# Opening of layer 0 in chunks of 2, 2, 4, 4, 2 and 2 k tiles, with the gate matrices loaded behind it

## The chip, the cores and the metric

One core of one Trainium2 chip. The metric is the time of one execution on the device, in microseconds (us), the median of three runs. One further execution was recorded by the profiler; all rows below are from it.

## What is computed

Two mixer layers over 256 latent and 256 context tokens of width 2048, then a last RMSNorm. All in float32. What matters here is how a layer begins:

```python
shift, scale, gate = jnp.split(c_act @ w_ada + b_ada, 3, axis=-1)
h = rmsnorm(x, norm_g) * (1 + scale) + shift
u = h @ w_in
```

`w_ada` is 2048 x 6144 for each layer, and the vectors `c_act` and `cc_act` (latent and context tokens) are multiplied by it. The 2048 inputs of `h` are 16 k tiles of 128. Behind it come a Conformer convolution, a gated linear recurrence (RG-LRU, whose small gate matrices are block diagonal), attention, and the output product.

## The kernel before

Everything is transposed: channels on the 128 partitions, the 512 tokens along the free axis. The product with `w_in` runs in blocks of 128 output columns, over 16 k tiles. Each float32 factor is split in two fp32r parts, and three matmuls of 128x512 are made per block and k tile (lines 559 to 561 in the opening, 614 to 616 behind it): high times high, high of the weights with low of h, low of the weights with high of h. ScalarE makes the high part of the weights (`w_hi`, line 803), VectorE subtracts it for the low part (`w_lo`, line 1077), in units of up to 1024 columns; there are 4 buffers for units, and the w_hi of unit u waits until the matmuls of unit u - 4 are done.

**The opening of layer 0.** The first seven blocks cannot wait for all of `c_act @ w_ada`. So they are made together, k tiles outside, each block in a PSUM bank of its own. A chunk is 2 k tiles of all seven blocks; 8 chunks. For a chunk these steps follow each other:

- `ada0_mm` (L512, matmuls at L523): `c_act` times the columns of `w_ada` of the chunk's k tiles, for scale and shift, in 4 pieces of 1 MB (scale 0 and 1, then shift 0 and 1), summed in one bank. A piece is here 1024 rows by 256 columns, 8 matmuls of 256 columns, each 1 KB run of memory one row of the transfer.
- ScalarE copies that bank (`ada0_rows`, L817), TensorE transposes it (`ada0_tp`, L531), VectorE sums and adds the bias (`ada0_out`, L1085 to L1096).
- For each k tile, VectorE makes `T` (L1128), ScalarE `h_hi` (L844), VectorE `h_lo` (L1135).
- The chunk's weights, one load of 896 KB (7 blocks by 256 columns), make two units, of 4 and of 3 blocks.
- TensorE runs 14 steps (`mm_chunk`, L542), a step being one block and one k tile: blocks 0 to 3 for both k tiles, then 4 to 6. Behind steps 1 and 3 it puts the two shift pieces of the *next* chunk, behind step 6 the transposes of the next chunk, behind steps 10 and 12 the two scale pieces of the chunk after that. `ada0_mm` for a chunk may start only when VectorE has summed the chunk before.

**The stream.** SyncE issues all weight loads from one list (`stream`, L158), in order. In the opening there are 40, numbered here from 0: per chunk three pieces, the weights, the last piece. They use 6 slots of 1 MB in rotation: three of `raw`, one in `glu`, two in `qreg`. So a load waits for the release of the load six before it (`used`, L309): for a piece its matmuls, for a chunk's weights the w_lo of the last unit made from them. Behind the opening the stream goes on with three slots (load 40 is the weights of block 7, load 41 those of block 8). There a piece of `w_ada` is 128 rows by 2048 columns, in 8 KB rows, and takes 4 matmuls of 512 columns (L501, 8 instructions); the opening of layer 1, at about 870 us, loads its weights in 2 KB rows. A waiting issue holds up all issues behind it. The matrices of the gates of the recurrence (`gate_weights`, L412, issues at L420, 4 loads of 128 KB in 256-byte rows) are issued behind load 32.

**VectorE's and ScalarE's order in a chunk.** VectorE: sums, T of the first k tile, w_lo of the first unit, T of the second, both h_lo, w_lo of the second unit. ScalarE: the copy of the bank, w_hi of the first unit, h_hi, w_hi of the second, h_hi.

The release of a chunk of weights and the slots, as the code has them:

```python
SLOT = [i % (NRAW + 3) if i < opened else (i - opened) % NRAW for i in range(len(STREAM))]
if SLOT[i] in SLOT[:i]:
    sp.wait_ge(*used(i - 1 - SLOT[:i][::-1].index(SLOT[i])))
if item[0] == "chunk":
    return C.at("lo", chunk_unit(item[1], False))
```

Of the kernel before, what the change touches and what calls it, by code (L numbers as in the profile page):

```python
# [21 lines left out]
ALU = mybir.AluOpType  # L22
# [42 lines left out]
CK = 2  # L65
CHUNKS = DT // CK
FRONT = 4
# [54 lines left out]
LEAD = 2  # L122
ADA0_AT, TP_AT, LEAD_AT = (1, 3), 6, (10, 12)


def ada0(c):

    return [("ada0", kind, c, g) for kind in (SCL, SHIFT) for g in range(2)]
# [6 lines left out]

SHIFTED = 2 * CHUNKS - 2 * OPEN[0]

# [6 lines left out]
def chunk_unit(c, front):  # L144

    return 2 * c + (0 if front else 1)
# [5 lines left out]


def chunk_blocks(front):
    return range(FRONT) if front else range(FRONT, OPEN[0])


def stream():  # L158

    plan = ada_plan()  # L160
    s = []
    for c in range(CHUNKS):
        first = ada0(c)
        s += first[:3] + [("chunk", c)] + first[3:]
    s += [("w", b) for b in (OPEN[0], OPEN[0] + 1)]
    for l in range(LAYERS):
        for b in range(OPEN[l], NB):
# [44 lines left out]
def program(nc, io, known):  # L212
    ctx = ExitStack()
    with ctx:
# [94 lines left out]
        def used(i):  # L309

            item = STREAM[i]
            if item[0] == "w":
                return C.at("lo", unit(0, item[1], 1))
            if item[0] == "chunk":
                return C.at("lo", chunk_unit(item[1], False))
            if item[0] == "open":
                return C.at("lo", quarter_unit(item[1], SIDE // 2 - 1))
            if item[0] == "pw":
                return C.at("pw_mm", item[1], CT - 1)
            return C.at(item[0] + "_mm", *item[1:])  # L320

        def source(u):

            if u < 2 * CHUNKS:
                c, back = divmod(u, 2)
                return ("chunk", c), slice(back * FRONT * CK * P, (OPEN[0] if back else FRONT) * CK * P)
# [6 lines left out]
        def block_done(gb):  # L333

            l, b = divmod(gb, NB)
            if b >= OPEN[l]:
                return C.at("mm", unit(l, b, 1))
            return C.at("mm", quarter_unit(3, b // 2) if l else chunk_unit(CHUNKS - 1, b < FRONT))
# [69 lines left out]
        def _(sp):  # L408
# [22 lines left out]
            for i, item in enumerate(STREAM):  # L431
# [5 lines left out]
                elif item[0] == "chunk":  # L437
                    src = io["w_blocks"][0:OPEN[0], :, item[1] * CK * P:(item[1] + 1) * CK * P].rearrange("b p c -> p b c")
                    dst = dst[:, 0:OPEN[0] * CK * P].rearrange("p (b c) -> p b c", b=OPEN[0])
# [4 lines left out]
                elif item[0] == "ada0":  # L444
                    kind, c, g = item[1:]
                    at0 = kind * D + c * CK * P
                    src = io["w_ada"][0, g * D // 2:(g + 1) * D // 2, at0:at0 + CK * P].rearrange("(j p) c -> p j c", p=P)
                    dst = dst.rearrange("p (j c) -> p j c", j=DT // 2)
# [9 lines left out]
                if i == 2 * DT:  # L458
                    gate_weights(0)
# [30 lines left out]
        def _(pe):  # L490
# [21 lines left out]
            def ada0_mm(kind, c, g):  # L512
# [4 lines left out]
                n = CK * P  # L517
# [3 lines left out]
                for j in range(8):  # L521
                    r = 32 * (j % 4)
                    last = mm(psA[r:r + 32, 0:n], rows[:, g * 8 + j, :], w[:, j * n:(j + 1) * n],  # L523
                              start=(kind == SCL and g == 0 and j < 4), stop=(kind == SHIFT and g == 1 and j >= 4),
                              tile_position=(0, r))
                last.then_inc(*C.up("ada0_mm", kind, c, g))

            def ada0_tp(c):
                pe.wait_ge(*C.at("ada0_rows", c))
                for j in range(CK):  # L530
# [11 lines left out]
            def mm_chunk(c):  # L542
# [3 lines left out]
                for front in (True, False):  # L546
                    u = chunk_unit(c, front)
                    pe.wait_ge(*C.at("lo", u))
                    for i in range(CK):
                        k = c * CK + i  # L550
                        if front:
                            pe.wait_ge(*C.at("h_lo", 0, k))
                        for n, b in enumerate(chunk_blocks(front)):
# [3 lines left out]
                            at = (n * CK + i) * P  # L557
# [177 lines left out]
            for item in ada0(1)[:LEAD]:  # L735
# [58 lines left out]
        def _(act):  # L794
# [20 lines left out]
            def ada0_rows(c):  # L815
                act.wait_ge(*C.at("ada0_mm", SHIFT, c, 1))
                fn(T[:, 6, 0:CK * P], psA[:, 0:CK * P], ACT.Copy).then_inc(*C.up("ada0_rows", c))  # L817
# [145 lines left out]
            for gb in range(GLOB):  # L963
                l, b = divmod(gb, NB)
                if b == 0:
# [3 lines left out]
                    if l == 0:  # L969
                        rms_std(l)  # L970
                        for c in range(CHUNKS):
                            if c:
                                ada0_rows(c)
                            hi(chunk_unit(c, True))
                            if c == 0:
                                hi(chunk_unit(c, False))
                                ada0_rows(c)
                            modulate(l, c * CK)
                            if c:
                                hi(chunk_unit(c, False))  # L980
                            modulate(l, c * CK + 1)
# [79 lines left out]
        def _(dve):  # L1061
# [18 lines left out]
            def ada0_out(c):  # L1080

                dve.wait_ge(*C.at("ada0_tp", c))
                ps = psA[:, 0:CK * P].rearrange("p (q j r) -> p r q j", q=CK, j=4)
                for kind, rows in ((SCL, slice(0, 2)), (SHIFT, slice(2, 4))):
                    V.tensor_reduce(tiny[:, 1 + kind, 0:2 * CK].rearrange("p (r q) -> p r q", r=2), ps[:, rows], axis=AX.X,  # L1085
                                    op=ALU.add).then_inc(*C.up("ada0_sum", kind, c))
                dve.wait_ge(*C.ago("ada0_sum"))
                for kind in (SCL, SHIFT):
                    at = kind * DT + c * CK
                    for i in range(2):  # L1090
                        V.tensor_tensor(ada[:, 0, i, at:at + CK], tiny[:, 1 + kind, CK * i:CK * i + CK], b_ada[:, 0, at:at + CK],
                                        ALU.add).then_inc(*C.up("ada_out", 0, kind, c))
# [401 lines left out]
```

## Time and profile before

| | |
|---|---|
| median of 3 runs | 1322.59 us (1319.38 to 1323.63) |
| the profiled execution | 1322.9 us, its span 1321.1 us |
| TensorE matmul busy | 1258.6 us, 95% of the span |
| VectorE, ScalarE busy | 733.7 us (56%), 534.6 us (40%) |
| share of TensorE in the chain that ended last | 83% |
| moved by DMA | 233.73 MB, mean 177 GB/s |

How to read it: times are us from the start of the span. The chain of waits follows, from the last instruction back, what released each step. A row of a timeline has start, duration, engine, line, operation, output and inputs, the count, and in brackets the idle time before it with what ended it. The duration of a matmul reaches to its modelled end; the distance between two starts is what one takes in a row of them. The granted clock of TensorE is given as a share of 2.4 GHz.

### The profile page before, as it was taken

What the parts mean: (1) busy time and instruction counts of PE and PEld (TensorE: products, weight loads), DVE (VectorE), ACT (ScalarE), POOL (GpSimd) and SP (SyncE); (2) the same over time, 40 slices, a digit from 0 to 9 for tenths busy, and PEclk for the clock granted to TensorE, in tenths of its full rate; (3) what the DMA queues carried; (4) which work ended last, traced back from release to release, by engine and by line L of the source; (5) the groups of instructions that cost most, each with busy time, mean ns of one, the idle gap of its engine ahead of it and who ended that gap; (6) DMA issues with size and microseconds to landing.
All of it is one profiled execution on the core that took longest, in us unless ns stands there. A gap on an engine that the chain in (4) does not pass through costs nothing.

```text
span 1321.1 us, 17033 instructions
## 1 busy us (share of the span) xinstructions
PE 1258.6 (95%) x7004; PEld 970.9 (73%) x7004; DVE 733.7 (56%) x1188; ACT 534.6 (40%) x843; POOL 8.2 (1%) x10
## 2 busy tenths in 40 slices
PE   3798999999999999999999999989999999999996
PEld 1465777767777777776777777758887998889995
DVE  3443436687565555552343233385789976755554
ACT  5222344452223334453332122244665554565452
POOL 0000100000000000000000000000000000000000
PEclk9999999999999999999999999989999999999998
DMA  9999655446443333333454554453332433325541
GB/s 343 332 320 324 220 201 212 191 192 263 155 187 128 128 127 127 128 128 134 169 225 175 213 208 173 186 191 104 120 131 93 160 128 128 128 96 192 182 169 64
DMA packets 76317, 233.73 MB, mean 177 GB/s; under 512 B 8016, under 2 KB 50128, under 8 KB 54352
## 3 DMA queue, kind: packets, MB, share of 16 engines
q1 hardware_dynamic: 76240, 232.65, 49.0%
q8 instruction: 55, 0.90, 0.3%
q14 instruction: 22, 0.18, 0.0%
HBM read 230.54 MB, written 2.10 MB: 176 GB/s over the span
## 4 chain that ended last, share of the span: by engine, by line
PE 83%; DVE 7%; DMA 5%; ACT 3%; issue 1%; SPq 0%; DVEq 0%; ACTq 0%
PE psum_block L614 21%; PE psum_block L615 20%; PE psum_block L616 20%; PE psum_ada L501 5%; PE psum_scores L691 3%; PE psum_scores L648 2%; PE psum_scores L669 2%; DMA raw<-in_w_ada 2%; DVE w_lo L1077 2%; DMA Y<-in_xT 1%; PE psum_scores L682 1%; DMA qreg<-in_w_ada 1%; DVE T L1128 1%; DVE h_lo L1135 1%; DMA glu<-in_w_ada 1%
## 5 line engine op out<-in xcount | busy, mean ns | idle before, releaser
L614 PE MATMUL psum_block<-h_hi,w_hi 128*128 128x512 f32 (+1 forms) x1616 | 562.4, 348 | 0.7 <-ACT glu L1050 0.7
L615 PE MATMUL psum_block<-h_lo,w_hi 128*128 128x512 f32 (+1 forms) x1616 | 547.9, 339 | 0.0
L616 PE MATMUL psum_block<-h_hi,w_lo 128*128 128x512 f32 (+1 forms) x1616 | 547.7, 339 | 0.0
L1077 DVE TENSOR_TENSOR w_lo<-raw,w_hi 128x1024 fp32r<-128x1024 f32 x218 | 263.4, 1218 | 398.6 <-ACT w_hi L803 398.4
L803 ACT ACTIVATE w_hi<-raw 128x1024 fp32r<-128x1024 f32 x218 | 228.5, 1053 | 530.1 <-PE psum_block L616 516.2
L614 PEld LDWEIGHTS psum_block<-h_hi,w_hi 128*128 128x128 f32 x1616 | 306.3, 190 | 78.1 <-issue 38.7
L615 PEld LDWEIGHTS psum_block<-h_lo,w_hi 128*128 128x128 f32 x1616 | 306.6, 190 | 35.3 <-issue 3.8
L616 PEld LDWEIGHTS psum_block<-h_hi,w_lo 128*128 128x128 f32 x1616 | 306.4, 190 | 34.2
L1276 DVE SCALAR_TENSOR_TENSOR Y<-glu,small,Y 128x512 f32<-128x512 f32 (+1 forms) x240 | 130.4, 612 | 0.0
L501 PE MATMUL psum_ada<-raw,cstat 128*32 128x512 f32 x512 | 67.2, 616 | 5.4 <-DMA raw<-in_w_ada 5.4
L917 ACT ACTIVATE T<-psum_scores,stats 128x512 f32<-128x512 f32 (+1 forms) x48 | 28.9, 615 | 52.7 <-DVE stats L1301 52.7
L844 ACT ACTIVATE h_hi<-T,ada 128x256 fp32r<-128x256 f32 x64 | 28.7, 501 | 45.4 <-DVE T L1128 45.4
L1085 DVE TENSOR_REDUCE tiny<-psum_ada 128x4 f32<-128x16 f32 x16 | 2.0, 169 | 71.3 <-PE psum_ada L531 71.3
L523 PE MATMUL psum_ada<-raw,cstat 128*32 128x256 f32 x272 | 20.5, 424 | 21.1 <-DMA raw<-in_w_ada 21.1
L691 PE MATMUL psum_scores<-T,v 128*128 128x512 f32 x80 | 36.4, 593 | 1.4 <-ACT T L932 1.4
L501 PEld LDWEIGHTS psum_ada<-raw,cstat 128*32 128x32 f32 x512 | 11.5, 109 | 34.5 <-issue 26.5
L831 ACT ACTIVATE T<-Y 128x512 f32<-128x512 f32 (+1 forms) x48 | 26.1, 550 | 22.4 <-DVE Y L1201 13.3
L648 PE MATMUL psum_scores<-T,bd 128*128 128x512 f32 x64 | 30.7, 625 | 3.9 <-DVE T L1234 3.9
L923 ACT ACTIVATE T<-T,stats 128x512 f32<-128x512 f32 (+1 forms) x48 | 27.3, 640 | 13.6 <-DVE stats L1311 13.6
L1234 DVE SCALAR_TENSOR_TENSOR T<-qreg,small,T 128x512 f32<-128x512 f32 x48 | 32.5, 745 | 0.0
L523 PEld LDWEIGHTS psum_ada<-raw,cstat 128*32 128x32 f32 x272 | 7.7, 118 | 32.5 <-issue 16.1
L669 PE MATMUL psum_scores<-kT,qreg 128*128 128x512 f32 x64 | 31.4, 611 | 0.0
(174 smaller groups left out, 1105.6 us busy)
## 6 DMA issues: line engine op xcount, KB each, us to landing
raw<-in_w_blocks SPq DMA_DIRECT2D x105, 1024.0 KB, 4.8
raw<-in_w_ada SPq DMA_DIRECT2D x81, 1024.0 KB, 5.5
qreg<-in_w_ada SPq DMA_DIRECT2D x10, 1024.0 KB, 11.2
glu<-in_w_ada SPq DMA_DIRECT2D x5, 1024.0 KB, 9.7
Y<-in_xT SPq DMA_DIRECT2D x4, 1024.0 KB, 12.4
T<-in_xT SPq DMA_DIRECT2D x16, 256.0 KB, 7.2
raw<-in_w_blocks SPq DMA_DIRECT2D x4, 896.0 KB, 11.4
raw<-in_pw SPq DMA_DIRECT2D x2, 1024.0 KB, 6.2
```

Source lines behind the costliest of these rows:

```text
L501: last = mm(psA[32 * j:32 * j + 32, :], cstat[:, k, 2:34], w[:, j * TOK:(j + 1) * TOK], start=(k == 0), stop=(k == DT - 1), tile_position= ...
L614: mm(ps[:, 0:n], hi, hh[:, k, t], start=(at == 0), stop=False)
L615: mm(ps[:, 0:n], hi, hl[:, k, t], start=False, stop=False)
L616: last = mm(ps[:, 0:n], lo, hh[:, k, t], start=False, stop=(at == DT - 1))
L648: last = mm(psS[:, 2 * d + g, :], bd[:, g, d * CT + t, :], T[:, 4 * d, :], start=True, stop=True)
L669: mm(psS[:, g, :], qt, kT[:, kv, :], start=True, stop=False)
L691: last = mm(psS[:, 0, :], v[:, kt, kv * HD:(kv + 1) * HD], T[:, 4 + kt, :], start=(kt == first), stop=(kt == 3))
L803: fn(wh[:, u % 4, 0:cols.stop - cols.start], raw_of(item)[:, cols], ACT.Copy).then_inc(*C.up("hi", u))
L917: fn(T[:, g, k0:TOK], psS[:, g, k0:TOK], ACT.Exp, scale=SCALE, bias=st[:, 1, g:g + 1], accum_out=st[:, 2, g:g + 1]).then_inc(*C.up("att_ex ...
L1077: V.tensor_tensor(wl[:, u % 4, 0:n], raw_of(item)[:, cols], wh[:, u % 4, 0:n].bitcast(F32), ALU.subtract).then_inc(*C.up("lo", u))
L1234: stt(out, x, lcw[:, c, k:k + 1], out, ALU.mult, ALU.add).then_inc(*C.up("taps", l, t, d))
L1276: stt(out, x, dwh[:, c:c + 1], out, ALU.mult, ALU.add).then_inc(*C.up("conv", l, t, k))
```

## The change

The opening is cut in 6 chunks of 2, 2, 4, 4, 2 and 2 k tiles. In a chunk of 4, a piece of `w_ada` is 512 rows by 512 columns (2 KB rows, 4 matmuls of 512 columns), and there are 8 pieces; the weights are two loads, blocks 0 to 3 (1 MB) and 4 to 6 (768 KB), in 2 KB rows too, and make four units, of 2, 2, 2 and 1 blocks. Chunks of 2 are loaded as before. There are again 40 loads: 0 to 9 as before; 10 to 15, 18 and 19 the pieces of chunk 2, 16 and 17 its weights; 20 to 25, 28 and 29 the pieces of chunk 3, 26 and 27 its weights; then two chunks of 5 loads.

`beside` places the pieces among TensorE's steps: the scale pieces of the chunk after next from 4 steps behind the transposes on, one a step; the shift pieces of the next chunk spread over the steps ahead of the transposes. This gives, for chunks 0 to 4: shift at steps 2, 4; 1, 2, 3, 4; 4, 8, 12, 16; 6, 13; 2, 4. Transposes behind step 6; 6; 20; 20; 6. Scale at 10 to 13; 10 to 13; 24, 25; 24, 25; none.

VectorE takes w_lo of the first unit ahead of the sums, and all the other w_lo of the chunk behind its last h_lo. ScalarE takes w_hi of the second unit behind the second h_hi. The gate matrices are issued behind load 40.

```diff
-CK = 2
-CHUNKS = DT // CK
-FRONT = 4
+SPAN = (2, 2, 4, 4, 2, 2)
+CHUNKS = len(SPAN)
+LOADS = {2: (range(0, 7),), 4: (range(0, 4), range(4, 7))}
+WORK = {2: (range(0, 4), range(4, 7)), 4: (range(0, 2), range(2, 4), range(4, 6), range(6, 7))}
+UNITS0 = [(c, n) for c in range(CHUNKS) for n in range(len(WORK[SPAN[c]]))]
...
-LEAD = 2
-ADA0_AT, TP_AT, LEAD_AT = (1, 3), 6, (10, 12)
...
-    return [("ada0", kind, c, g) for kind in (SCL, SHIFT) for g in range(2)]
+    return [("ada0", kind, c, g) for kind in (SCL, SHIFT) for g in range(SPAN[c])]
...
-SHIFTED = 2 * CHUNKS - 2 * OPEN[0]
+SHIFTED = len(UNITS0) - 2 * OPEN[0]
...
-def chunk_unit(c, front):
-    return 2 * c + (0 if front else 1)
+def chunk_k(c):
+    return sum(SPAN[:c])
+def chunk_unit(c, n):
+    return UNITS0.index((c, n))
+def chunk_units(c):
+    return range(chunk_unit(c, 0), chunk_unit(c, 0) + len(WORK[SPAN[c]]))
+def beside(c):
+    tp = OPEN[0] * SPAN[c] - 8
+    late = ada0(c + 1)[SPAN[c + 1]:] if c + 1 < CHUNKS else []
+    ahead = ada0(c + 2)[:SPAN[c + 2]] if c + 2 < CHUNKS else []
+    steps = {(i + 1) * tp // (len(late) + 1): item for i, item in enumerate(late)}
+    steps.update({tp + 4 + i: item for i, item in enumerate(ahead)})
+    return tp, steps
...
-        s += first[:3] + [("chunk", c)] + first[3:]
+        early = len(first) - SPAN[c] // 2
+        s += first[:early] + [("chunk", c, n) for n in range(len(LOADS[SPAN[c]]))] + first[early:]
...
-                return C.at("lo", chunk_unit(item[1], False))
+                c, blocks = item[1], LOADS[SPAN[item[1]]][item[2]]
+                return C.at("lo", max(chunk_unit(c, n) for n, w in enumerate(WORK[SPAN[c]]) if w[0] in blocks))
...
-            if u < 2 * CHUNKS:
-                c, back = divmod(u, 2)
-                return ("chunk", c), slice(back * FRONT * CK * P, (OPEN[0] if back else FRONT) * CK * P)
+            if u < len(UNITS0):
+                c, n = UNITS0[u]
+                blocks, cols = WORK[SPAN[c]][n], SPAN[c] * P
+                m = next(m for m, load in enumerate(LOADS[SPAN[c]]) if blocks[0] in load)
+                first = blocks[0] - LOADS[SPAN[c]][m][0]
+                return ("chunk", c, m), slice(first * cols, (first + len(blocks)) * cols)
...
-                    src = io["w_blocks"][0:OPEN[0], :, item[1] * CK * P:(item[1] + 1) * CK * P].rearrange("b p c -> p b c")
-                    dst = dst[:, 0:OPEN[0] * CK * P].rearrange("p (b c) -> p b c", b=OPEN[0])
+                    blocks, cols, at0 = LOADS[SPAN[item[1]]][item[2]], SPAN[item[1]] * P, chunk_k(item[1]) * P
+                    src = io["w_blocks"][blocks[0]:blocks[-1] + 1, :, at0:at0 + cols].rearrange("b p c -> p b c")
+                    dst = dst[:, 0:len(blocks) * cols].rearrange("p (b c) -> p b c", b=len(blocks))
...
-                    at0 = kind * D + c * CK * P
-                    src = io["w_ada"][0, g * D // 2:(g + 1) * D // 2, at0:at0 + CK * P].rearrange("(j p) c -> p j c", p=P)
-                    dst = dst.rearrange("p (j c) -> p j c", j=DT // 2)
+                    rows, cols, at0 = D // SPAN[c], SPAN[c] * P, kind * D + chunk_k(c) * P
+                    src = io["w_ada"][0, g * rows:(g + 1) * rows, at0:at0 + cols].rearrange("(j p) c -> p j c", p=P)
+                    dst = dst.rearrange("p (j c) -> p j c", c=cols)
...
-                if i == 2 * DT:
+                if item == ("w", OPEN[0]):
                     gate_weights(0)
...
-                n = CK * P
+                n, count = SPAN[c] * P, DT // SPAN[c]
                 rows = cstat[:, :, 2:34] if kind == SCL else cstat[:, :, 0:32]
                 if g == 0 and kind == SCL and c:
                     pe.wait_ge(*C.at("ada0_sum", SHIFT, c - 1))
-                for j in range(8):
+                for j in range(count):
                     r = 32 * (j % 4)
-                    last = mm(psA[r:r + 32, 0:n], rows[:, g * 8 + j, :], w[:, j * n:(j + 1) * n],
-                              start=(kind == SCL and g == 0 and j < 4), stop=(kind == SHIFT and g == 1 and j >= 4),
-                              tile_position=(0, r))
+                    last = mm(psA[r:r + 32, 0:n], rows[:, g * count + j, :], w[:, j * n:(j + 1) * n],
+                              start=(kind == SCL and g == 0 and j < 4),
+                              stop=(kind == SHIFT and g == SPAN[c] - 1 and j >= count - 4), tile_position=(0, r))
...
                 step = 0
-                for front in (True, False):
-                    u = chunk_unit(c, front)
+                tp, steps = beside(c)
+                for u, blocks in zip(chunk_units(c), WORK[SPAN[c]]):
                     pe.wait_ge(*C.at("lo", u))
-                    for i in range(CK):
-                        k = c * CK + i
-                        if front:
+                    for i in range(SPAN[c]):
+                        k = chunk_k(c) + i
+                        if blocks[0] == 0:
                             pe.wait_ge(*C.at("h_lo", 0, k))
-                        for n, b in enumerate(chunk_blocks(front)):
+                        for n, b in enumerate(blocks):
                             if k == 0 and b == 2:
                                 pe.wait_ge(*C.at("rms_std", 0))
                             ps = bank(b)
-                            at = (n * CK + i) * P
+                            at = (n * SPAN[c] + i) * P
                             hi, lo = wh[:, u % 4, at:at + P], wl[:, u % 4, at:at + P]
                             mm(ps, hi, hh[:, k, :], start=(k == 0), stop=False)
                             mm(ps, hi, hl[:, k, :], start=False, stop=False)
                             last = mm(ps, lo, hh[:, k, :], start=False, stop=(k == DT - 1))
-                            if i == CK - 1 and b == chunk_blocks(front)[-1]:
+                            if i == SPAN[c] - 1 and b == blocks[-1]:
                                 last.then_inc(*C.up("mm", u))
-                            if step in ADA0_AT and c + 1 < CHUNKS:
-                                ada0_mm(*ada0(c + 1)[LEAD + ADA0_AT.index(step)][1:])
-                            if step == TP_AT and c + 1 < CHUNKS:
+                            if step in steps:
+                                ada0_mm(*steps[step][1:])
+                            if step == tp and c + 1 < CHUNKS:
                                 ada0_tp(c + 1)
-                            if step in LEAD_AT and c + 2 < CHUNKS:
-                                ada0_mm(*ada0(c + 2)[LEAD_AT.index(step)][1:])
                             step += 1
...
                         for c in range(CHUNKS):
-                            if c:
-                                ada0_rows(c)
-                            hi(chunk_unit(c, True))
-                            if c == 0:
-                                hi(chunk_unit(c, False))
-                                ada0_rows(c)
-                            modulate(l, c * CK)
-                            if c:
-                                hi(chunk_unit(c, False))
-                            modulate(l, c * CK + 1)
+                            units = chunk_units(c)
+                            hi(units[0])
+                            ada0_rows(c)
+                            for i in range(2):
+                                modulate(l, chunk_k(c) + i)
+                            hi(units[1])
+                            for i in range(2, SPAN[c]):
+                                modulate(l, chunk_k(c) + i)
+                                hi(units[i])
...
             def h_chunk(c):
-                k = c * CK
-                if k:
-                    dve.wait_ge(*C.at("h_lo", 0, k - 1))
-                modulate(0, k)
-                lo(chunk_unit(c, True))
-                modulate(0, k + 1)
+                for k in range(chunk_k(c), chunk_k(c) + SPAN[c]):
+                    if k >= 2:
+                        dve.wait_ge(*C.at("h_lo", 0, k - 2))
+                    modulate(0, k)
+                    if k > chunk_k(c):
+                        h_lo(0, k - 1)
                 h_lo(0, k)
-                h_lo(0, k + 1)
-                lo(chunk_unit(c, False))
...
                         for c in range(CHUNKS):
+                            lo(chunk_units(c)[0])
                             ada0_out(c)
                             h_chunk(c)
+                            for u in chunk_units(c)[1:]:
+                                lo(u)
```

The sums of `ada0_out` and the copy of `ada0_rows` take the width of the chunk in the same way.

## Rows read from the trace of the kernel before

**Rows 1.** The page, part 2: GB/s in 40 slices of 33 us

```profile
GB/s 343 332 320 324 220 201 212 191 192 263 155 187 128 128 127 127 128 128 134 169 225 175 213 208 173 186 191 104 120 131 93 160 128 128 128 96 192 182 169 64
```

**Rows 2.** TensorE's waits from 38 to 164 us; engines' busy time from 164 to 857 us

```profile
PE psum_ada L523 <- DMA raw<-in_w_ada: 5.1, 4, 2.2
PE psum_ada L523 <- DMA qreg<-in_w_ada: 4.2, 2, 3.4
PE psum_ada L523 <- DMA glu<-in_w_ada: 3.3, 2, 2.9
...
164.00:857.00 693.00, 693.00 (x3172) 500.98 (x3174) 345.47 (x488) 241.28 (x378) 1.85 (x1) 1.00 0.46 174
```

**Rows 3.** Waits of SyncE's DMA queue from 38 to 164 us

```profile
SPq L454 <- DVE w_lo L1077: 56.0, 9, 11.4
```

**Rows 4.** The chain from 67 us on: start, duration, what

```profile
66.97 0.27 DVE tiny L1085 x2
...
67.94 0.88 DVE T L1128 x2
68.82 1.14 DVE w_lo L1077
69.96 0.79 DVE T L1128 x2
70.75 1.58 DVE h_lo L1135 x4
72.33 0.88 DVE w_lo L1077
...
73.23 5.39 DMA raw<-in_w_ada
...
119.69 8.25 DMA qreg<-in_w_ada
```

**Rows 5.** TensorE's timeline in chunk 3: start, duration, what

```profile
100.47 1.07 PE L523 MATMUL psum_ada<-raw,cstat 128*32 128x256 f32 x16
...
102.06 0.40 PE L561 MATMUL psum_scores<-h_hi,w_lo 128*128 128x512 f32 x1
102.29 0.40 PE L559 MATMUL psum_scores<-h_hi,w_hi 128*128 128x512 f32 x1
...
103.08 1.07 PE L523 MATMUL psum_ada<-raw,cstat 128*32 128x256 f32 x16
```

**Rows 6.** The chain behind the opening: two pieces of 512 columns

```profile
175.26 1.85 PE psum_ada L501 x16
```

**Rows 7.** DMA in 40 slices of 56 to 120 us, then of 868 to 874 us

```profile
GB/s 252 268 371 355 350 348 349 346 348 348 94 108 372 359 356 349 349 349 348 348 266 264 380 352 349 349 350 353 348 349 141 328 373 350 349 350 346 350 294 203
...
GB/s 437 382 382 423 437 396 382 382 382 328 205 273 341 341 396 396 382 423 396 355 410 382 396 355 382 451 410 451 273 232 314 259 396 55 546 55 601 109 710 164
```

**Rows 8.** The chain's transfers at 56 and 141 us; landing of the load issued at 157.9

```profile
56.27 7.05 DMA raw<-in_w_ada
...
140.57 5.21 DMA glu<-in_w_ada
...
DMA to landing us min/median/max: 5.1/5.1/5.1
```

**Rows 9.** TensorE after two idles (timeline), the chain at 134 us, granted clock at 128

```profile
46.41 1.07 PE L523 MATMUL psum_ada<-glu,cstat 128*32 128x256 f32 x16 [2.94 <-DMA glu<-in_w_ada]
...
127.98 1.94 PE L523 MATMUL psum_ada<-qreg,cstat 128*32 128x256 f32 x16 [3.38 <-DMA qreg<-in_w_ada]
...
134.05 0.23 PE psum_ada L531 x2
...
128.00:130.00 2.00, 2.00 (x17) 0.73 (x17) 0.00 (x0) 0.01 (x1) 0.00 (x0) 0.50 1.10 349
```

**Rows 10.** The first matmul of block 7 on TensorE

```profile
163.77 0.39 PE L614 MATMUL psum_block<-h_hi,w_hi 128*128 128x512 f32 x1
```

**Rows 11.** The issues of the gate matrices: duration ns min/median/max

```profile
L420 SPq DMA_DIRECT2D bd<-in_lru_w x4: 1352/1676/2942, 109.8 to 116.2; - x4
```

More of the change, by code:

```diff
@@ L118, in ada_plan @@
     return plan
-LEAD = 2
-ADA0_AT, TP_AT, LEAD_AT = (1, 3), 6, (10, 12)
 def ada0(c):
-    return [("ada0", kind, c, g) for kind in (SCL, SHIFT) for g in range(2)]
+    return [("ada0", kind, c, g) for kind in (SCL, SHIFT) for g in range(SPAN[c])]
 def opening(quarter):
     return [("open", quarter)]
-SHIFTED = 2 * CHUNKS - 2 * OPEN[0]
+SHIFTED = len(UNITS0) - 2 * OPEN[0]
 def unit(l, b, j):
     return SHIFTED + 2 * (l * NB + b) + j
-def chunk_unit(c, front):
-    return 2 * c + (0 if front else 1)
+def chunk_k(c):
[11 more added lines that the diff above has]
+    return tp, steps
 def quarter_unit(quarter, pair):
     return unit(1, 0, 0) + quarter * SIDE // 2 + pair
-def chunk_blocks(front):
-    return range(FRONT) if front else range(FRONT, OPEN[0])
 def stream():
@@ L337, in block_done @@
                 return C.at("mm", unit(l, b, 1))
-            return C.at("mm", quarter_unit(3, b // 2) if l else chunk_unit(CHUNKS - 1, b < FRONT))
+            if l:
+                return C.at("mm", quarter_unit(3, b // 2))
+            last = CHUNKS - 1
+            return C.at("mm", chunk_unit(last, next(n for n, w in enumerate(WORK[SPAN[last]]) if b in w)))
         def bank(gb):
@@ L529, in ada0_tp @@
                 pe.wait_ge(*C.at("ada0_rows", c))
-                for j in range(CK):
+                for j in range(SPAN[c]):
                     last = nc.tensor.transpose(psA[:, j * P:(j + 1) * P], T[:, 6, j * P:(j + 1) * P], ident)
@@ L734, in _ @@
             ada0_tp(0)
-            for item in ada0(1)[:LEAD]:
+            for item in ada0(1)[:SPAN[1]]:
                 ada0_mm(*item[1:])
@@ L815, in ada0_rows @@
             def ada0_rows(c):
-                act.wait_ge(*C.at("ada0_mm", SHIFT, c, 1))
-                fn(T[:, 6, 0:CK * P], psA[:, 0:CK * P], ACT.Copy).then_inc(*C.up("ada0_rows", c))
+                act.wait_ge(*C.at("ada0_mm", SHIFT, c, SPAN[c] - 1))
+                fn(T[:, 6, 0:SPAN[c] * P], psA[:, 0:SPAN[c] * P], ACT.Copy).then_inc(*C.up("ada0_rows", c))
             def square(l, m):
@@ L1082, in ada0_out @@
                 dve.wait_ge(*C.at("ada0_tp", c))
-                ps = psA[:, 0:CK * P].rearrange("p (q j r) -> p r q j", q=CK, j=4)
+                n, k = SPAN[c], chunk_k(c)
+                ps = psA[:, 0:n * P].rearrange("p (q j r) -> p r q j", q=n, j=4)
                 for kind, rows in ((SCL, slice(0, 2)), (SHIFT, slice(2, 4))):
-                    V.tensor_reduce(tiny[:, 1 + kind, 0:2 * CK].rearrange("p (r q) -> p r q", r=2), ps[:, rows], axis=AX.X,
+                    V.tensor_reduce(tiny[:, 1 + kind, 0:2 * n].rearrange("p (r q) -> p r q", r=2), ps[:, rows], axis=AX.X,
                                     op=ALU.add).then_inc(*C.up("ada0_sum", kind, c))
@@ L1088, in ada0_out @@
                 for kind in (SCL, SHIFT):
-                    at = kind * DT + c * CK
+                    at = kind * DT + k
                     for i in range(2):
-                        V.tensor_tensor(ada[:, 0, i, at:at + CK], tiny[:, 1 + kind, CK * i:CK * i + CK], b_ada[:, 0, at:at + CK],
+                        V.tensor_tensor(ada[:, 0, i, at:at + n], tiny[:, 1 + kind, n * i:n * i + n], b_ada[:, 0, at:at + n],
                                         ALU.add).then_inc(*C.up("ada_out", 0, kind, c))
-                ck = slice(c * CK, (c + 1) * CK)
                 dve.wait_ge(*C.ago("ada_out"))
                 for i in range(2):
-                    stt(A[:, 0, i, ck], ada[:, 0, i, SCL * DT + c * CK:SCL * DT + (c + 1) * CK], 1.0,
-                        norm_g[:, 0, ck], ALU.add, ALU.mult).then_inc(*C.up("A", 0, i))
+                    stt(A[:, 0, i, k:k + n], ada[:, 0, i, SCL * DT + k:SCL * DT + k + n], 1.0,
+                        norm_g[:, 0, k:k + n], ALU.add, ALU.mult).then_inc(*C.up("A", 0, i))
                 dve.wait_ge(*C.ago("A"))
```

## The prediction

> **What bounds the kernel now.** I read the slices of the page first. The first four, 132 us and nearly all of the opening of layer 0, move 320 to 343 GB/s, where the later ones mostly move 60 to 260 [rows 1]: only here is the DMA near what it can bring. The waits say what that costs: from 38 to 164 us TensorE waits for pieces of w_ada for 5.1 + 4.2 + 3.3 = 12.6 us, and from 164 to 857 us it is busy for 693.00 of 693.00 us [rows 2]. So what the opening gains or loses reaches the end of the kernel whole: nothing behind it can take time back.
>
> Who holds the transfers up is in SyncE's waits: 56.0 us for w_lo in the opening [rows 3]. A load takes the slot of the load six before it. The slot of a piece of w_ada comes free with its matmuls, but that of a chunk of weights only with VectorE's last w_lo from it, behind the whole modulation of that chunk. The chain of chunk 2 shows this ring: sums from 66.97, modulation, the last w_lo at 72.33, the issue at 73.23, landing 5.39 us later [rows 4]. Three turns take from 73.23 to 119.69, 15.5 us each, and TensorE's own work in a chunk is 14 steps of 0.69, four pieces of 1.22 and 0.26 of transposes, 14.8 us. The step is three matmuls 0.23 apart; the piece is 103.08 - 100.47 less two steps [rows 5]. So at present the load that waits for w_lo is the last piece of the next chunk, one per turn, and the turn hides nearly all of it.
>
> **The prices.** A piece of 512 columns: two take 1.85 us, so 0.93, and with the 0.15 that a lone piece has on top of its 1.07 it is 1.08 (0.15 is 1.22 less the row's 1.07) [rows 5, 6]. A megabyte in 1 KB rows goes at 349 GB/s, 3.0 us; in 2 KB rows (the opening of layer 1) mostly at 382 to 396, 2.65 us [rows 7]. A load that finds the queue empty lands 5.2 to 5.4 us after its issue, one in 8 KB rows after 5.1 [rows 4, 8]; I take 5.1 for 2 KB rows and 5.4 for 1 KB rows. The clock: after an idle of 3.38 us TensorE ran at 1.2 GHz from 127.98 to 134.05, 6.1 us, and lost 3.0; after 2.94 us it lost nothing, the piece behind it took the 1.07 of the full clock [rows 9]. VectorE from the transposes to the last w_lo: now 6.26 us (66.97 to 73.23). A chunk of 2 k tiles has w_lo of 1.14 in front instead, and the second w_hi behind both h_hi, so 5.6. A chunk of 4 needs, up to the w_lo that ends the first weight load, 0.97 for the sums, 4 x 0.83 of T, 4 x 0.79 of h_lo, about 1.2 of waits for h_hi and 1.14 of w_lo: 9.8 us [rows 4].
>
> **The new order.** The loads are numbered from 0 as they are issued. Up to load 9 they are the same; 10 to 19 are chunk 2 (16 and 17 its weights), 20 to 29 chunk 3, 30 on chunks 4 and 5. Two things change for slots. Load 14, still behind w_lo of chunk 1, is now one of eight pieces that TensorE wants *during* chunk 1 (14, 15, 18, 19 at its steps 1 to 4). And loads 22 and 23, the pieces that TensorE wants at steps 12 and 13 of chunk 1, take the slots of 16 and 17: the weights of chunk 2, which are not released until chunk 2 is modulated.
>
> - Chunk 0: load 9 lands at 46.6 (46.4 now, a w_hi later), its piece ends 47.8, two steps and the transposes 49.4, then 7 steps and 4 pieces: 58.6. Loads 10 to 13 land by 46.6 + 4 x 2.65 = 57.2. Load 14 is issued at 49.4 + 5.6 = 55.0 and lands 59.9; then 15 at 62.5, 16 65.2, 17 (three quarters) 67.2, 18 69.8, 19 72.5.
> - Chunk 1: at step 3, 64.3, TensorE waits for load 18 until 69.8: **5.5 us idle**. Pieces, three steps and transposes would end at 75.2; at the low clock 77.3.
> - Load 22 waits for w_lo of chunk 2: 77.3 + 9.8 = 87.1, landing 92.2. TensorE is at that piece at 77.3 + 6 x 0.69 + 2 x 1.08 = 83.6: **8.6 us idle**.
> - Piece and step 13 at the low clock end at 95.7. Only now may ScalarE overwrite the w_hi buffer of the fourth unit of chunk 2; w_hi and w_lo of 512 columns are 0.65 each, load 23 is issued at 97.0 and lands at 102.1: **6.4 us idle**. Its piece ends at 104.2.
> - Chunk 2: 28 x 0.69 + 4 x 1.08 + 2 x 1.22 + 0.26 + 2.0 of low clock = 28.4, to 132.6, no wait (load 29 lands by 102.1 + 5.75 x 2.65 = 117.3).
> - Chunk 3: load 32 waits for chunk 3's first weights: transposes at 125.3, + 9.8 + 5.4 = 140.5; TensorE is there at 137.4, 3.1 us idle. Then 21 steps, 4 pieces, transposes: 160.2.
> - Chunk 4: 12.4, to 172.6. Chunk 5: 14 steps, 9.7, to 182.3. Block 7 now begins at 163.77 [rows 10], so the opening is **18.5 us longer**.
>
> **The gate matrices.** Their four small loads (issues of up to 2.94 us [rows 11]) stand between loads 32 and 33 and make one turn, from 119.69 to 140.57, 20.9 instead of 15.5 us, clock included [rows 4, 8]; that 5.4 us is saved and is already in the sum above, which has no such hole. In their new place they go out at about 160 and are first used behind block 8, which begins 11 us (16 steps) after 182.3. Behind them stands load 41, the weights of block 8: issued by about 168, it lands by 174. Cost nothing. The reorder of w_hi and w_lo in chunks of 2 costs nothing beyond the 0.2 above.
>
> The profiled execution took 1322.9, of it 1321.1 span; the median is 0.3 lower. 1322.6 + 18.5 = **1341 us**.
>
> **Bounds.** Row rate: 3.0 us per MB (no better than now) adds 3.1 in chunk 1 and little later; 410 GB/s takes 1. Lone landing: up to 7.05 [rows 8] adds 2 to 5, less where loads queue. Clock: if the idles of 3.1 us too drop it, 3 more; if none does, 6 to 7 less. So 1334 to 1349 for this case.
>
> The Trainium skill (DMA: Bandwidth & Descriptors, Anatomy of one DMA) fits a GpSimd-issued DMA as 2.0 us plus bytes by 436 GB/s, an estimate of 4.4 us for 1 MB: by that the three lone landings would give 2 us back, 1339. The rows show 5.1 at best, and the sum goes by them.
>
> **Rivals.**
> 1. *Slots do not bind; the rate does.* Then the 5.4 us of the gate loads go, at most 6.3 us of the other waits (12.6 less 3.4 of that turn and the first 2.9), and 16 x 0.14 of pieces: 1309 at best, about **1313**. For it: the DMA is full for most of the opening. Against it: 56.0 us of SyncE's waits are w_lo, and loads 22 and 23 are later in the slot order than chunk 2's weights. It decides if these two are issued before 75 us. 7 in 100. This is the other side; within 0.3% (about what a measurement can tell from no change), 2 in 100.
> 2. *The waits come, the clock holds.* 3.38 us is the only drop of the opening, and it may be chance. **1335**, 12 in 100.
> 3. *2 KB rows run like 1 KB rows.* Loads 10 to 19 then take 3.0 us per MB and the first idle is 8.6: **1344**, 5 in 100, since 382 to 396 GB/s stands in the rows against 349. (The Trainium skill, same page, Specifications, puts line rate at 512 B and more, by which doubling 1 KB rows brings nothing; the trace disagrees.)
> 4. The sum as above, 74 in 100.
>
> Faster 0.07, same 0.02, slower 0.91. The range leaves out rival 1 and the same-time case, and takes the bounds of the rest: 1332 to 1350.
>
> **What would show it.** In the profile after: SyncE waits for w_lo in two long stretches, about 20 us before load 22 (near 87) and some 9 before load 23; TensorE idle for w_ada near 64 to 70, 84 to 92, 96 to 102 and 137 to 140, some 24 us in all; 1.2 GHz after each of the first three; DMA almost idle from about 78 to 87; block 7 beginning near 182; no gate load in the opening. It is wrong if TensorE's idle in chunk 1 is under 10 us, or if block 7 begins before 164.

## The result and the profile after

| kernel | median us | against the kernel before (95% interval) |
|---|---|---|
| before, beside it | 1321.46 (1319.38 to 1323.63) | |
| changed | 1342.23 (1340.42 to 1343.38) | 1.0156 (1.0136 to 1.0175) |

The change makes the kernel 20.8 us slower. The page of the changed kernel, part 2 (TensorE's granted clock in tenths, and GB/s, in 40 slices of 33.5 us):

```profile
PEclk9978999999999999999999999989999999999998
...
GB/s 345 341 171 275 272 165 228 221 188 226 214 188 126 126 126 151 130 107 148 141 237 172 187 212 211 179 183 94 158 98 91 158 147 137 126 95 180 175 180 63
```

Against [rows 1] the high rates of the opening now spread over five slices instead of four, and the third slice moves 171 GB/s where its neighbours move 341 and 275. The clock is down in slices 3 and 4 (0.7 and 0.8). TensorE's and SyncE's waits in the opening (in all, how often, the longest):

```profile
PE psum_ada L544 <- DMA qreg<-in_w_ada: 14.3, 2, 7.5
PE psum_ada L544 <- DMA raw<-in_w_ada: 7.6, 2, 5.5
PE psum_ada L544 <- DMA glu<-in_w_ada: 5.2, 2, 3.4
```

```profile
SPq L475 <- DVE w_lo L1095: 84.6, 9, 19.7
SPq L475 <- PE psum_ada L544: 18.7, 9, 3.8
```

There are 27.1 us of waits for w_ada (14.3 + 7.6 + 5.2) instead of 12.6 [rows 2], and 84.6 us of SyncE's waits for w_lo instead of 56.0 [rows 3]. TensorE's timeline, the pieces it waited for and the first matmul of block 7:

```profile
46.66 1.20 PE L544 MATMUL psum_ada<-glu,cstat 128*32 128x256 f32 x16 [3.44 <-DMA glu<-in_w_ada]
...
65.73 1.06 PE L544 MATMUL psum_ada<-glu,cstat 128*32 128x512 f32 x8 [1.74 <-DMA glu<-in_w_ada]
...
73.19 1.93 PE L544 MATMUL psum_ada<-raw,cstat 128*32 128x512 f32 x8 [5.50 <-DMA raw<-in_w_ada]
...
94.54 1.93 PE L544 MATMUL psum_ada<-qreg,cstat 128*32 128x512 f32 x8 [7.51 <-DMA qreg<-in_w_ada]
...
104.80 1.94 PE L544 MATMUL psum_ada<-qreg,cstat 128*32 128x512 f32 x8 [6.75 <-DMA qreg<-in_w_ada]
...
141.75 1.07 PE L544 MATMUL psum_ada<-raw,cstat 128*32 128x256 f32 x16 [2.09 <-DMA raw<-in_w_ada]
...
184.45 0.39 PE L633 MATMUL psum_block<-h_hi,w_hi 128*128 128x512 f32 x1
```

These are loads 9, 15, 18, 22, 23 and 32. A duration of 1.93 for a piece is the low clock, one of 1.07 the full; behind the pieces at 46.66 and 141.75 the clock fell a little after they began. Block 7 begins at 184.45, 20.7 us behind [rows 10], and in the 693 us behind it nothing changes: TensorE is busy for 693.00 us again, as in [rows 2]; that is the last line here (each line: busy time of PE, PEld, DVE, ACT, POOL, granted clock, DMA share, GB/s):

```profile
48.00:50.00 2.00, 2.00 (x5) 1.61 (x6) 0.00 (x0) 0.29 (x1) 0.00 (x0) 0.50 1.05 387
74.00:76.00 2.00, 2.00 (x10) 0.83 (x3) 0.00 (x0) 0.00 (x0) 0.00 (x0) 0.50 1.05 386
80.00:84.00 4.00, 4.00 (x25) 2.54 (x23) 3.37 (x14) 1.56 (x4) 0.00 (x0) 1.00 0.01 4
84.00:88.00 4.00, 3.02 (x18) 1.13 (x14) 3.94 (x10) 3.64 (x7) 0.00 (x0) 1.00 0.00 2
144.00:146.00 2.00, 2.00 (x6) 1.63 (x5) 0.00 (x0) 0.00 (x0) 0.00 (x0) 0.50 1.05 349
184.00:877.00 693.00, 693.00 (x3171) 501.44 (x3173) 344.90 (x487) 241.46 (x378) 1.85 (x1) 1.00 0.46 174
```

The granted clock is 0.50, 1.2 GHz, behind the idles, and from 80 to 88 us the DMA moves almost nothing (4 and 2 GB/s) while TensorE runs dry at 87. Why stands in the chain of waits and in the timeline of VectorE and ScalarE:

```profile
58.82 14.32 DMA raw<-in_w_ada
...
88.20 1.15 DVE w_lo L1095
89.36 5.13 DMA qreg<-in_w_ada
...
99.53 5.23 DMA qreg<-in_w_ada
...
135.35 1.15 DVE w_lo L1095
136.51 5.20 DMA raw<-in_w_ada
```

```profile
80.51 0.29 DVE L1104 TENSOR_REDUCE tiny<-psum_ada 128x8 f32<-128x32 f32 x2 [9.79 <-PE psum_ada L552]
...
98.15 0.63 ACT L822 ACTIVATE w_hi<-qreg 128x512 fp32r<-128x512 f32 x1 [10.50 <-PE psum_misc L582]
98.81 0.69 DVE L1095 TENSOR_TENSOR w_lo<-qreg,w_hi 128x512 fp32r<-128x512 f32 x1 [8.34 <-ACT w_hi L822]
```

The sums of chunk 2 begin at 80.51; behind its modulation VectorE makes the w_lo that releases the first load of weights, from 88.20 on; only then, at 89.36, load 22 is issued, and it lands 5.13 us later. (The row at 58.82 is load 18, to which the section on the prediction comes back.) Load 23 waits for the w_lo at 98.81, which waits for the w_hi at 98.15, which waited 10.5 us for TensorE's last step of chunk 1. Load 32 repeats the first of these at 135.35. This is the ring of [rows 4] with one difference: what now stands six loads behind the weights of chunk 2 is a piece that TensorE wants before chunk 2 begins.

Last, the transfers of 56 to 80 us, nearly all in 2 KB rows:

```profile
GB/s 24 14 55 113 331 382 413 403 440 375 389 386 393 382 389 389 386 393 389 386 386 389 382 382 386 386 389 386 393 386 389 386 396 382 382 382 389 382 174 24
```

That is mostly 382 to 393, about 386 GB/s or 2.72 us for 1 MB, against 349 in 1 KB rows [rows 7].

### The profile page after: what moved, and what is told of

Same layout as the page of the kernel before. It is cut to its first block, busy times and chain, and to the rows that moved or that the text cites. A ratio compares the mean times of both kernels' runs of the same rounds, so it can differ in the third digit from the quotient of the medians.

```text
span 1341.2 us, 16753 instructions
## 1 busy us (share of the span) xinstructions
PE 1263.2 (94%) x6876; PEld 969.3 (72%) x6876; DVE 733.4 (55%) x1172; ACT 534.3 (40%) x841; POOL 8.2 (1%) x10
## 4 chain that ended last, share of the span: by engine, by line
PE 85%; DVE 5%; DMA 4%; ACT 3%; issue 1%; SPq 0%; DVEq 0%; ACTq 0%
PE psum_block L633 20%; PE psum_block L634 20%; PE psum_block L635 20%; PE psum_ada L522 4%; PE psum_scores L710 3%; PE psum_scores L688 2%; PE psum_scores L667 2%; DMA raw<-in_w_ada 2%; PE psum_ada L544 2%; DMA Y<-in_xT 1%; PE psum_scores L701 1%; PE psum_scores L580 1%; PE psum_scores L581 1%; PE psum_scores L582 1%; DVE w_lo L1095 1%
## 5 line engine op out<-in xcount | busy, mean ns | idle before, releaser
L544 PE MATMUL psum_ada<-raw,cstat 128*32 128x256 f32 (+1 forms) x224 | 23.1, 524 | 23.2 <-DMA raw<-in_w_ada 23.2
L1256 DVE SCALAR_TENSOR_TENSOR qreg<-qreg,T 128x512 f32<-128x512 f32 x16 | 10.3, 688 | 36.1 <-ACT qreg L922 36.1
```

Of the source, the lines that this page charges most:

```text
L544: last = mm(psA[r:r + 32, 0:n], rows[:, g * count + j, :], w[:, j * n:(j + 1) * n], start=(kind == SCL and g == 0 and j < 4), stop=(kind = ...
```

## The experiments

Theory: the weights of a chunk of 4 sit in the slots that pieces of the next chunk need (two long idles and a short one), and chunk 1 wants twice the pieces before its transposes (one idle); the low clock adds to both. The rivals are named with each run. Each ratio below is to the kernel before, run beside that experiment on the same chip; its median there was 1321.8 (e1 to e4), 1322.8 (e5, e6, e8, e9) and 1322.7 (e10), against 1321.46 beside the change. "The change" is 1342.23, and differences to it are differences of medians, so they are good to 1 or 2 us only.

**e1, the gate matrices alone.** The kernel before, with

```diff
-                if i == 2 * DT:
+                if item == ("w", OPEN[0]):
                     gate_weights(0)
```

> The kernel before with one edit: the gate matrices are issued behind load 40, as in the change. Theory (slot ring, the gate loads being a hole of their own): the turn of 20.9 us becomes 15.5, about 5.5 us less than before, 1316. Rival (the gate loads were hidden beside the ring, TensorE's wait there had another cause): 1321 to 1322.

1317.63 us, 0.9972 (0.9961 to 0.9984): 4.2 us less (2 to 5 by the interval), and not the 5.5 expected. From its timeline, the piece of load 9, and block 7:

```profile
45.90 1.94 PE L523 MATMUL psum_ada<-glu,cstat 128*32 128x256 f32 x16 [3.04 <-DMA glu<-in_w_ada]
...
159.35 0.39 PE L614 MATMUL psum_block<-h_hi,w_hi 128*128 128x512 f32 x1
```

The gate hole is gone. Block 7 begins at 159.35, 4.4 us earlier than [rows 10]. The clock fell behind the first idle, of 3.04 us instead of 2.94 [rows 9], but that cost little here: the piece of load 14 comes at 63.83 instead of 63.37, since its own wait shrank from 2.19 to 0.37 us. The two turns around the hole, from the piece at 109.84 to the one at 145.82, took 36.0 us, and take 31.2 in e1 (110.23 to 141.41): 4.8 us are gained, and 0.4 lost ahead of them. Of the 5.4 priced, 0.6 comes back as a wait, since the piece at 145.82 waited 0.33 us and the one at 141.41 waits 0.90.

**e2, no chunks of 4.** The changed kernel with

```diff
-SPAN = (2, 2, 4, 4, 2, 2)
+SPAN = (2, 2, 2, 2, 2, 2, 2, 2)
```

> The changed kernel with SPAN all 2: new orders of w_hi and w_lo, steps 2, 4, 10 and 11 for the pieces, gates behind, but no chunk of 4. Theory (only the slots of the weights of chunks of 4 and the eight pieces asked for in chunk 1 cost): 1312 to 1315, under e1, since w_lo is released earlier. Rival (the new order of w_lo and w_hi, or the new steps, cost part of the 20 us): 1325 or more. Rival (rows of 2 KB are worth much): slower than e1.

1315.08 us, 0.9943 (0.9930 to 0.9956), 27 less than the change. The new orders of w_hi and w_lo, the new steps and the new place of the gate matrices cost nothing together: all the loss is in the chunks of 4.

**e3, slots of their own for the weights.** The changed kernel with

```diff
-        SLOT = [i % (NRAW + 3) if i < opened else (i - opened) % NRAW for i in range(len(STREAM))]
+        chunks = [i for i in range(opened) if STREAM[i][0] == "chunk"]
+        pieces = [i for i in range(opened) if STREAM[i][0] != "chunk"]
+        SLOT = [(i - opened) % NRAW for i in range(len(STREAM))]
+        for n, i in enumerate(chunks):
+            SLOT[i] = NRAW + 1 + n % 2
+        for n, i in enumerate(pieces):
+            SLOT[i] = n % (NRAW + 1)
```

> The changed kernel, chunks of 4 included, with two slots of their own for the weights and four for the pieces of w_ada. Theory: the idles before loads 22, 23 and 32 go (7.5, 6.8 and 2.1 us, with the clock behind them), the idle of 5.5 us before load 18 stays: about 23 us less than the change, 1319. Rival (the DMA rate, or the work of four k tiles on VectorE, holds chunk 1 up): 1335 or more.

1319.88 us, 0.9985 (0.9976 to 0.9994): 22.4 us less than the change. All the pieces that TensorE waits for, and block 7:

```profile
46.21 1.07 PE L550 MATMUL psum_ada<-glu,cstat 128*32 128x256 f32 x16 [2.77 <-DMA glu<-in_w_ada]
...
62.44 1.06 PE L550 MATMUL psum_ada<-raw,cstat 128*32 128x512 f32 x8 [0.47 <-DMA raw<-in_w_ada]
...
69.83 1.94 PE L550 MATMUL psum_ada<-raw,cstat 128*32 128x512 f32 x8 [5.44 <-DMA raw<-in_w_ada]
...
159.54 0.39 PE L639 MATMUL psum_block<-h_hi,w_hi 128*128 128x512 f32 x1
```

The idles before loads 22, 23 and 32 are gone; the one before load 18 is still there with 5.44 us, and the low clock behind it. It ends at 69.83 instead of 73.19, since load 14 no longer waits for w_lo either. Block 7 comes 24.9 us earlier: 16.4 are the three idles (7.51 + 6.75 + 2.09), 3.4 the earlier load 18, and the remaining 5.2 the clock behind those idles, an estimate by difference. The chunks of 4, their sizes, steps and rows were not touched. This is the run that decides.

**e4 and e10, own slots without chunks of 4.** e4 is e3 with the SPAN of e2; e10 is e1 with the SLOT of e3, so the kernel before with two edits.

> SPAN all 2 and the slots of e3. Theory: the w_lo no longer holds any piece up, TensorE is the bound from 50 us on: 1311 to 1314, within 2 us of e2, in which that wait is nearly hidden already. Rival (four slots for pieces are too few): slower than e2 by over 3 us.

> The kernel before with two edits: the gate matrices behind the opening as in e1, and two slots for the weights and four for the pieces as in e3. Theory: w_lo holds no piece up, whatever the order of w_lo in a chunk, so the time is that of e4, 1311 to 1314. Rival (the new orders of w_hi and w_lo are what makes e4 faster than e1): 1316 or more.

e4: 1311.41 us, 0.9929 (0.9916 to 0.9943). e10: 1311.77 us, 0.9920 (0.9903 to 0.9937). Both beat both kernels, by 10 us and by 30. All of e4's waits for w_ada in the opening:

```profile
PE psum_ada L550 <- DMA raw<-in_w_ada: 0.7, 1, 0.7
PE psum_ada L550 <- DMA glu<-in_w_ada: 0.2, 1, 0.2
```

0.9 us is left of 12.6 [rows 2]. Where weights and pieces do not share slots, the order of w_lo within a chunk no longer matters, as e10 shows. e4 is 3.7 us under e2 where at most 2 were expected. In the profiled executions only 1.3 of it lie in the opening (block 7 of e2, then of e4):

```profile
153.58 0.39 PE L633 MATMUL psum_block<-h_hi,w_hi 128*128 128x512 f32 x1
```

```profile
152.31 0.39 PE L639 MATMUL psum_block<-h_hi,w_hi 128*128 128x512 f32 x1
```

The rest came behind block 7, which neither edit touches; five executions of e2 went from 1311.3 to 1315.7. The four runs e2, e3, e4 and the change together say more than e3 alone: slots of their own are worth 1.3 to 3.7 us with chunks of 2 (e2 to e4) and 22.4 with chunks of 4 (the change to e3). And even with slots of their own, chunks of 4 stay 8.5 us slower than chunks of 2 (e3 against e4): the idle before load 18 and the clock behind it are most of that.

**e8, w_lo early.** The changed kernel; in a chunk of 4, w_hi and w_lo of the first two units go ahead of the sums on both engines (ScalarE's part first):

```diff
-                            hi(units[0])
+                            early = SPAN[c] // 2
+                            for u in units[:early]:
+                                hi(u)
...
-                            hi(units[1])
+                            if early < 2:
+                                hi(units[1])
...
-                            lo(chunk_units(c)[0])
+                            early = SPAN[c] // 2
+                            for u in chunk_units(c)[:early]:
+                                lo(u)
                             ada0_out(c)
                             h_chunk(c)
-                            for u in chunk_units(c)[1:]:
+                            for u in chunk_units(c)[early:]:
                                 lo(u)
```

> The changed kernel with w_hi and w_lo of the first two units of a chunk of 4 ahead of its sums and modulation, so that the first of its two weight loads is released before it is modulated. Theory: loads 22 and 32 no longer wait, the idle of 7.5 us goes, that before load 23 (6.8 us, behind the matmuls of the fourth unit before) stays: 1329 to 1331. Rival (it is the DMA or the modulation itself that is late): 1340 or more.

1329.03 us, 1.0046 (1.0034 to 1.0058): 13.2 less than the change. The pieces of loads 9, 18 and 23, and block 7:

```profile
45.94 1.07 PE L544 MATMUL psum_ada<-glu,cstat 128*32 128x256 f32 x16 [1.59 <-DMA glu<-in_w_ada]
...
70.69 1.94 PE L544 MATMUL psum_ada<-raw,cstat 128*32 128x512 f32 x8 [6.58 <-DMA raw<-in_w_ada]
...
92.62 1.94 PE L544 MATMUL psum_ada<-qreg,cstat 128*32 128x512 f32 x8 [6.68 <-DMA qreg<-in_w_ada]
...
169.39 0.39 PE L633 MATMUL psum_block<-h_hi,w_hi 128*128 128x512 f32 x1
```

Load 22 is on time, load 23 (6.68 us) is not: w_hi at 86.04 behind TensorE's last step of chunk 1, w_lo at 86.70, the issue at 87.42. So these are two waits with two causes: the first is w_lo behind the modulation, the second w_hi behind the matmuls that use its buffer. Some 2.5 us of the gain in this execution are chance: load 18 came at 70.69 instead of 73.19, since the clock did not fall behind load 9.

**e9, the chunks of 4 last.** e3 with SPAN (2, 2, 2, 2, 4, 4).

> Own slots as in e3 and chunks of 2, 2, 2, 2, 4, 4. Theory: the idle of 5.4 us that stays in e3 belongs to the step from a chunk of 2 to one of 4 (eight pieces and two weight loads wanted by the transposes of chunk 1's successor) and moves with it: same time as e3, 1319, idle of 4 to 6 us at about 93 us. Rival (it comes from the slow start of the kernel's loads): gone, 1312 to 1314.

1318.24 us, 0.9967 (0.9954 to 0.9980), close to e3 (0.9985, 0.9976 to 0.9994); block 7 begins at 159.69, there at 159.54. The waiting pieces in its chunk 3:

```profile
91.86 1.06 PE L550 MATMUL psum_ada<-raw,cstat 128*32 128x512 f32 x8 [0.29 <-DMA raw<-in_w_ada]
...
99.31 1.93 PE L550 MATMUL psum_ada<-raw,cstat 128*32 128x512 f32 x8 [5.50 <-DMA raw<-in_w_ada]
```

The idle moved from 70 to 99 us and kept its size, 5.50. It belongs to the step from a chunk of 2 to one of 4, and not to the start of the kernel.

**e5, 1 KB rows.** The changed kernel; every load of a chunk of 4 as two DMAs of 256 columns each (`halves(i)` is 2 for those loads, else 1, and the waits count both; "..." marks what is left out):

```diff
...
-                sp.dma_start(dst, src).then_inc(C.sem(f"raw{SLOT[i]}"), 16)
+                for g in range(halves(i)):
+                    w = slice(g * 2 * P, (g + 1) * 2 * P)
+                    d, s = (dst[:, :, w], src[:, :, w]) if halves(i) == 2 else (dst, src)
+                    sp.dma_start(d, s).then_inc(C.sem(f"raw{SLOT[i]}"), 16)
```

> The changed kernel with each load of a chunk of 4 issued as two halves with 1 KB rows. Theory: the slots set the two long idles whatever the rows are, only the idle before load 18 grows, 5.5 to 8 or 9 us: about 3 us more than the change, 1345. Rival (2 KB rows carry the time): over 1350. Rival (rows are worth nothing here): 1342.

1345.28 us, 1.0160 (1.0140 to 1.0181), 3 us more than the change by the medians; by the ratios (1.0156 for the change) the two can't be told apart, so the size rests on the traces. Some of its waits, before loads 9, 13, 14, 15, 18, 22, 23 and 28:

```profile
46.15 1.07 PE L552 MATMUL psum_ada<-glu,cstat 128*32 128x256 f32 x16 [0.54 <-DMA glu<-in_w_ada]
...
58.19 1.06 PE L552 MATMUL psum_ada<-raw,cstat 128*32 128x512 f32 x8 [0.76 <-DMA raw<-in_w_ada]
...
61.20 1.06 PE L552 MATMUL psum_ada<-raw,cstat 128*32 128x512 f32 x8 [0.35 <-DMA raw<-in_w_ada]
...
64.63 1.06 PE L552 MATMUL psum_ada<-glu,cstat 128*32 128x512 f32 x8 [1.47 <-DMA glu<-in_w_ada]
...
72.92 1.94 PE L552 MATMUL psum_ada<-raw,cstat 128*32 128x512 f32 x8 [6.33 <-DMA raw<-in_w_ada]
...
93.80 1.94 PE L552 MATMUL psum_ada<-qreg,cstat 128*32 128x512 f32 x8 [7.63 <-DMA qreg<-in_w_ada]
...
104.06 1.94 PE L552 MATMUL psum_ada<-qreg,cstat 128*32 128x512 f32 x8 [6.75 <-DMA qreg<-in_w_ada]
...
120.50 1.35 PE L552 MATMUL psum_ada<-qreg,cstat 128*32 128x512 f32 x8 [2.27 <-DMA qreg<-in_w_ada]
```

The waits from load 13 to load 18 grow from 7.2 (1.74 + 5.50) to 8.9 us (0.76 + 0.35 + 1.47 + 6.33), and load 28, on time in the change, is waited for 2.27 us; 7.63 and 6.75 before loads 22 and 23 are the slots' and stay. Its waits in the whole opening are 28.2 us against 27.1, but load 9, which both kernels load alike, has 0.54 of them here and 3.44 there, and the clock did not fall behind it in e5. So e5 was 1.9 us ahead at the transposes of chunk 1 (48.65 against 50.52) and 2.8 us behind at block 7 (187.25 against 184.45): in these executions the wider rows gain 4.7 us, nearly all of it where transfers queue, and next to nothing where a slot is held.

**e6, the clock held.** The changed kernel with matmuls on a tile of zeros ahead of the waits, which add 0 to a bank:

```diff
+            FILL = {(SHIFT, 1, 1): 3, (SHIFT, 2, 2): 5, (SCL, 3, 2): 7, (SCL, 3, 3): 6, (SCL, 4, 2): 2, (SHIFT, 4, 0): 2}
+
             def ada0_mm(kind, c, g):
...
+                for i in range(FILL.get((kind, c, g), 0)):
+                    mm(pB[0][:, :], ones, bd[:, 0, 0:4, :], start=False, stop=False)
...
+            pe.wait_ge(*C.at("bd_zero"))
```

The entry (SCL, 4, 2) has no effect, since chunk 4 has no such piece; the last line makes TensorE wait until the tile is zero.

> The changed kernel with matmuls on zeros (they add 0 to the bank of block 0) in the idles before loads 9, 18, 22, 23 and 32: 3, 5, 7, 6 and 2 of them at 0.86 us each. The idles themselves stay, only the clock is held. Theory: 6 to 7 us of the loss are the low clock, 1335 to 1337. Rival (the clock was a small part, the matmuls on the path are not slowed much): 1341 or more.

1336.48 us, 1.0095 (1.0071 to 1.0119), 5.8 less than the change by the medians and 8 by the ratios; block 7 comes 6.9 us earlier. Loads 18, 22 and 23, and block 7:

```profile
71.83 1.07 PE L547 MATMUL psum_ada<-raw,cstat 128*32 128x512 f32 x8 [1.88 <-DMA raw<-in_w_ada]
...
91.56 1.07 PE L547 MATMUL psum_ada<-qreg,cstat 128*32 128x512 f32 x8 [1.40 <-DMA qreg<-in_w_ada]
...
100.25 1.06 PE L547 MATMUL psum_ada<-qreg,cstat 128*32 128x512 f32 x8 [1.56 <-DMA qreg<-in_w_ada]
...
177.57 0.39 PE L636 MATMUL psum_block<-h_hi,w_hi 128*128 128x512 f32 x1
```

Each of these pieces now takes 1.07 instead of 1.93, and everything behind it comes earlier. Doing useless work in the waits is worth 6 to 8 us of the 21; not waiting gives back all of it, as e3 shows.

## Why the prediction was right

1341 was forecast with 1332 to 1350, 1342.2 was measured. That the two are 1.2 us apart is in part luck: 18.5 us were forecast and 20.8 measured, and the sum began from a median of 1322.6 for the kernel before, which was 1321.5 beside the change. The steps, in the profiled execution:

| step | forecast | measured |
|---|---|---|
| piece of load 9 | 46.6 | 46.66 |
| load 14 issued | 55.0 | 56.5 |
| piece of load 18, idle before loads 15 and 18 | 69.8, 0 + 5.5 | 73.19, 1.74 + 5.50 |
| sums of chunk 2 | 77.3 | 80.51 |
| load 22 issued, its piece, idle | 87.1, 92.2, 8.6 | 89.36, 94.54, 7.51 |
| load 23 issued, its piece, idle | 97.0, 102.1, 6.4 | 99.53, 104.80, 6.75 |
| load 32: piece, idle | 140.5, 3.1 | 141.75, 2.09 |
| block 7 | 182.3 | 184.45 |
| SyncE's longest wait for w_lo | about 20 | 19.7 |

- *Two loads in the slots of chunk 2's weights*: right, and shown by e3, and for the first of them alone by e8. Taking it out in e3 gives back 22.4 us, more than the whole loss: e3 also has the gain of the gate matrices, and a load 14 that does not wait for w_lo, and against these the idle before load 18.
- *VectorE's 9.8 us for a chunk of 4*: measured 8.85 (80.51 to 89.36). The 1.2 us of waits for h_hi stand in no row, and none came: between 80.51 and 89.36 VectorE's trace shows no wait, ScalarE's h_hi ran beside it. This is the larger part of the 1.1 by which the idle before load 22 was smaller; for the rest, TensorE took 6.8 us and not 6.3 to get to that piece.
- *Load 9 costs nothing new*: its piece began at 46.66, as forecast, but the idle before it was 3.44 instead of 2.94 us, and the clock fell behind it (0.50 at 48 to 50 us). So the transposes of chunk 1 and with them load 14 came 1.5 us late. This is chance rather than the change: e2, e5 and e8 have the same first ten loads and steps, and there the idle was 1.34, 0.54 and 1.59 us and the piece ran at the full clock.
- *Loads 15 to 18 land 2.65 us apart behind load 14*: the weak step. Load 14 landed 5.1 us behind its issue, as priced (the sum has 4.9, a slip), but load 15, issued 0.4 us after it, landed 8.8 us behind its own, some 4.1 us after load 14. Hence the idle of 1.74 us, which the sum does not have, and 1.5 us more by which load 18 was late; with load 14's delay it came 3.4 late (issued at 58.82, landed 14.32 us later). Why load 15 took 4.1 and not 2.65 us was not tried, and stays open. VectorE's shorter chunks of 4 took a part of the 3.4 back, so that block 7 missed the forecast by 2.1.
- *The idle of 2.1 us before load 32*: the clock fell behind it too (0.50 at 144 to 146 us), which the sum left to its upper bound; block 7 lost 0.9 us more there (1.25 late at load 32, 2.15 at block 7).
- *2 KB rows at 2.65 us per MB*: 2.72; against 1 KB rows e5 gives them 3 us in the medians and 4.7 in the opening of the profiled executions.
- *The gate matrices, 5.4 us*: too high; e1 gives 4.8 in the trace and 4.2 in the medians.
- *The clock, 6 to 7 us*: e6 gives 6 to 8, with the idles not quite filled.
- *Nothing behind the opening takes time back*: right.

The rivals: that the slots do not bind fell in the profile (load 22 was issued at 89.36, not before 75) and with e3; that the clock holds, and that 2 KB rows run like 1 KB rows, fell in the profile. The Trainium skill (DMA: Bandwidth & Descriptors, Specifications) puts the least transfer for line rate at 512 B. The traces here disagree: 349 GB/s with 1 KB rows, 386 with 2 KB rows.

## What to carry to other kernels

In a ring of buffers filled in one order, ask of each load what released its slot, and not only whether the bandwidth suffices: a tile that is held through a long chain (here weights until a chunk is modulated) must not stand one turn ahead of a tile that this same chain, or the work ahead of it, needs soon. Give tiles of long and of short life slots of their own. Where chunks grow, the step from small to large needs the whole larger chunk's inputs within the time of the smaller one.

## What was not expected

The clock fell after an idle of 3.44 us in the changed kernel and of 3.04 in e1, and held after 2.94 in the kernel before; in the changed kernel it also fell after one of 2.09 us, while it held after 2.76 in e10 and 2.77 in e3. The length of the last idle alone does not tell which; what else does was not tried. What a drop costs the kernel depends on the wait that follows: it was priced at 3.0 us from [rows 9], but in e1, where it made TensorE reach the piece of load 14 2.3 us later than in the kernel before, the wait that stood there anyway took up all but 0.5 us. Nor is the idle before load 9 a property of the kernel: its piece began between 45.90 and 46.66 us in the kernel before, the changed one, e1, e2, e3, e5, e8 and e9, but the idle before it was anything from 0.54 to 3.44 us, by when TensorE got there.
